# Expert slots taken in pairs of a big and a small one, phase by phase, with fewer rows in all, and one test ahead of the overflow loop

## What is computed

```python
def swiglu(h, w_gate, w_up, w_down):
    return (jax.nn.silu(h @ w_gate) * (h @ w_up)) @ w_down

def moe_swiglu(h, router_w, w_gate, w_up, w_down):      # h: 256 tokens x 1024
    logits = xt @ router_w                               # 8 experts
    top_val, top_idx = lax.top_k(logits, 2)
    top_w = softmax(top_val)
    # each token goes through its two experts: 1024 -> 3584 (gate, up), silu(gate) * up, 3584 -> 1024
    # out[token] = sum over its two experts of top_w * swiglu(token)
    ...
x = x + g_f * moe_swiglu(...)
return rms_norm(x, final_g)
```

## Time and profile before

| | us |
|---|---|
| median of three runs | 1509.3 (1508.0 to 1511.3) |
| the profiled execution | 1512.6 |
| its span, first to last instruction | 1510.8 |
| TensorE busy | 1430.1 |
| VectorE / ScalarE busy | 405.9 / 304.2 |

### The profile page before, as it was taken

The page is one execution under the profiler, slowest core; times in us unless marked ns, Lnnn a source line. Parts: engine busy times, 40 slices in busy tenths (PEclk is TensorE's granted clock), DMA queues, the critical chain, the costliest instruction groups (busy, mean ns, idle before and its releaser), DMA issues.

```text
span 1510.8 us, 26562 instructions
## 1 busy us (share of the span) xinstructions
PE 1430.1 (95%) x11666; PEld 724.1 (48%) x11667; DVE 405.9 (27%) x759; ACT 304.2 (20%) x556; POOL 36.6 (2%) x86
## 2 busy tenths in 40 slices
PE   6999999999999989999977899999999999999795
PEld 5757888887685772343322333334333343333231
DVE  4867655554496651100000000000100000000003
ACT  2356444433235420010100100001010010001001
POOL 1011000000000200000000000000000000000010
PEclk9999999999999989999999999999999999999999
DMA  9988574555757978999999999766999999995796
GB/s 350 312 346 293 181 230 172 208 205 216 267 212 309 326 310 298 383 371 403 403 409 409 402 408 409 295 236 225 407 402 409 409 402 409 408 362 209 294 404 250
DMA packets 149166, 489.31 MB, mean 324 GB/s; under 512 B 9562, under 2 KB 12066, under 8 KB 143938
## 3 DMA queue, kind: packets, MB, share of 16 engines
q1 hardware_dynamic: 141922, 475.06, 81.7%
q10 hardware_dynamic: 5328, 8.05, 1.9%
q0 software_dynamic: 1808, 4.60, 1.0%
HBM read 479.42 MB, written 6.16 MB: 321 GB/s over the span
## 4 chain that ended last, share of the span: by engine, by line
PE 77%; SPq 10%; DMA 6%; DVE 4%; ACT 2%; issue 2%; POOL 0%; DVEq 0%; POOLq 0%; ACTq 0%
PE ps L2322 31%; PE ps L2362 14%; PE ps L2041 7%; PE ps L2043 7%; PE ps L2042 7%; SPq L704 6%; SPq L710 3%; DMA raw<-in_moe_w_down_dram 2%; DMA weights<-in_ada_w_dram 2%; PE ps L2294 1%; PE ps L1967 1%; DMA raw<-in_moe_w_up_dram 1%; DVE weights_lo L1200 1%; PE ps L2339 1%; PE ps L2122 1%
## 5 line engine op out<-in xcount | busy, mean ns | idle before, releaser
L2322 PE MATMUL ps<-raw,hX 128*32 128x512 f32 (+1 forms) x5248 | 570.9, 592 | 27.2 <-DMA raw<-in_moe_w_up_dram 17.3
L2322 PEld LDWEIGHTS ps<-raw,hX 128*32 128x32 f32 x5248 | 168.4, 111 | 403.3 <-issue 370.7
L2362 PE MATMUL ps<-raw,m_actT 128*32 128x512 f32 x2240 | 248.8, 592 | 12.8 <-DMA raw<-in_moe_w_down_dram 12.0
L2041 PE MATMUL ps<-weights_hi,hT_hi 128*128 128x512 f32 (+1 forms) x416 | 162.1, 390 | 2.6 <-DVE hT_lo L1303 1.4
L2043 PE MATMUL ps<-weights_hi,hT_lo 128*128 128x512 f32 (+1 forms) x416 | 159.0, 382 | 0.0
L2042 PE MATMUL ps<-weights_lo,hT_hi 128*128 128x512 f32 (+1 forms) x416 | 158.7, 381 | 0.0
L2362 PEld LDWEIGHTS ps<-raw,m_actT 128*32 128x32 f32 x2240 | 72.8, 110 | 175.9 <-issue 163.3
L1596 DVE TENSOR_TENSOR m_act<-m_sg,ps 128x512 f32<-128x512 f32 (+2 forms) x32 | 23.5, 735 | 465.5 <-ACT m_sg L1034 465.5
L1200 DVE TENSOR_TENSOR weights_lo<-weights,weights_hi 128x2048 fp32r<-128x2048 f32 (+1 forms) x52 | 113.1, 2202 | 2.3 <-ACT weights_hi L873 1.1
L1594 DVE TENSOR_TENSOR m_actX<-m_sgX,ps 128x256 f32<-128x256 f32 (+1 forms) x12 | 4.7, 388 | 368.4 <-ACT m_sg L1034 368.4
L873 ACT ACTIVATE weights_hi<-weights 128x2048 fp32r<-128x2048 f32 (+1 forms) x48 | 87.2, 1839 | 55.6 <-PE ps L2043 51.3
(11 more groups left out here) (246 smaller groups left out, 1017.1 us busy)
## 6 DMA issues: line engine op xcount, KB each, us to landing
raw<-in_moe_w_gate_dram SPq DMA_DIRECT2D x112, 1024.0 KB, 15.4
raw<-in_moe_w_up_dram SPq DMA_DIRECT2D x112, 1024.0 KB, 17.9
raw<-in_moe_w_down_dram SPq DMA_DIRECT2D x112, 1024.0 KB, 16.1
weights<-in_ada_w_dram SPq DMA_DIRECT2D x20, 2048.0 KB, 9.8
weights<-in_ffn_w_gate_dram SPq DMA_DIRECT2D x14, 1024.0 KB, 6.3
weights<-in_ffn_w_up_dram SPq DMA_DIRECT2D x14, 1024.0 KB, 8.9
weights<-in_ffn_w_down_dram SPq DMA_DIRECT2D x7, 2048.0 KB, 10.4
weights<-in_w_in_dram SPq DMA_DIRECT2D x6, 2048.0 KB, 12.6
```

Of the source, the lines that this page charges most:

```text
L2041: pe.matmul(dst, stat_hi, hi, start=start, stop=False, skip_group_check=True)
L2322: mm = pe.matmul(ps[32 * q:32 * q + 32, bank, 0:2 * w].rearrange("p (g n) -> p g n", g=2), hX[:, z.rows_at, k, at32:at32 + 32], weights[:, ...
L2362: mm = pe.matmul(ps[32 * quarter:32 * quarter + 32, DOWN_BANK[c], 0:w], stationary[:, 32 * half:32 * half + 32], raw[buffer][:, D * j + w ...
```

## The change

The slots become "A", "ABX", "X", "AX", "X", "AB", "A", "A": eight wide passes and four X passes, 640 rows. Rank 1 (the largest expert) sits in slot 1 (160 rows), ranks 6 and 7 in the X slots 2 and 4 (32 rows), rank 3 in slot 3 (96), rank 2 in slot 5 (128), ranks 4 and 5 in slots 6 and 7 (64), rank 0 in slot 0 (64).

The slots are put in groups, (0), (1, 2), (3, 4), (5, 6), (7). Within a group the two slots are taken phase by phase in turn; `STEPS` lists the 32 steps, and the down sums of a step come behind the unit sums of the next step, which now belongs to the other slot. `chunk_order` follows, with the same 168 chunks and the same nine buffers. A group's rows are gathered and modulated together (up to 192 rows), so there are five gathers for eight before. PSUM banks of the down sums are given out by `DOWN_AT`; an X slot shares bank 7 with its partner, in the other half. Waits on semaphores count steps in place of slots and phases.

`MAX_OVER` is 5. Ahead of the overflow loop every engine loads one flag and skips the whole loop where it is 0.

```diff
-MAX_OVER = 4
+MAX_OVER = 5
-SLOT_RANK = (0, 4, 5, 1, 6, 3, 2, 7)
-SLOT_PASSES = ("AX", "A", "A", "ABX", "A", "AX", "AB", "A")
+SLOT_RANK = (0, 1, 6, 3, 7, 2, 4, 5)
+SLOT_PASSES = ("A", "ABX", "X", "AX", "X", "AB", "A", "A")
+GROUPS = ((0,), (1, 2), (3, 4), (5, 6), (7,))
-DOWN_BANK = {"A": 5, "B": 6, "X": 7}
+DOWN_AT = ({"A": (5, 0)}, {"A": (5, 0), "B": (6, 0), "X": (7, 0)}, {"X": (7, HU)}, {"A": (5, 0), "X": (7, 0)},
+           {"X": (7, HU)}, {"A": (5, 0), "B": (6, 0)}, {"A": (7, 0)}, {"A": (5, 0)})
+DOWN_FREE = (0, 1, 0, 3, 0, 4, 5, 6)
+GATHER_BANKS = ((2, 3, 6, 7), (0, 1, 2, 3), (0, 1, 2, 3), (4,))
+STEPS = [(s, n) for group in GROUPS for n in range(NPH) for s in group]
+def step_before(s, n):
+    p = STEPS.index((s, n))
+    return [STEPS[p - 1]] if p and (s, n) != (LAST, 0) else []
+def ended_by(s, n):
+    return step_before(s, n) + ([(s, n)] if n == NPH - 1 and s >= LAST - 1 else [])
 def chunk_order():
     order = []
-    for s in range(N_EXP):
-        for n in range(NPH):
-            order += [("gu", s, n, i) for i in range(GU_CHUNKS[n])]
...
+    for s, n in STEPS:
+        order += [("gu", s, n, i) for i in range(GU_CHUNKS[n])]
+        for t, m in ended_by(s, n):
+            order += [("down", t, m, i) for i in range(DOWN_CHUNKS[m])]
     return order
...
             def down_sums(sig, z, n):
-                pe.wait_ge(sig.copied, z.s * NPH + (n + 1))
-                if n == 0 and sig is main and z.s:
-                    pe.wait_ge(sig.y, z.s)
+                pe.wait_ge(sig.copied, z.at(n))
+                if n == 0 and z.down_free:
+                    pe.wait_ge(main.y, z.down_free)
+                if n == NPH - 1 and not z.starts:
+                    pe.wait_ge(main.y, z.s)
...
-            def slot(s):
-                z = MainSlot(s)
+            def step(s, n):
+                z, j = MainSlot(s), GROUP_OF[s]
...
-                pe.wait_ge(main.rows, s + 1)
-                unit_sums(main, z, 0)
-                if s not in (0, LAST):
-                    down_sums(main, MainSlot(s - 1), NPH - 1)
-                turn_units(main, z, 0)
-                for n in range(1, NPH):
-                    unit_sums(main, z, n, (next_rows if s < LAST else last_picks) if n == NPH - 1 else None)
-                    down_sums(main, z, n - 1)
-                    turn_units(main, z, n)
-                if s >= LAST - 1:
-                    down_sums(main, z, NPH - 1)
+                if (s, n) == (GROUPS[j][0], 0):
+                    pe.wait_ge(main.rows, j + 1)
+                ends = n == NPH - 1 and s == GROUPS[j][-1]
+                unit_sums(main, z, n, (next_rows if s < LAST else last_picks) if ends else None)
+                for t, m in step_before(s, n):
+                    down_sums(main, MainSlot(t), m)
+                turn_units(main, z, n)
+                if n == NPH - 1 and s >= LAST - 1:
+                    down_sums(main, z, n)
             def overflow():
-                with pe.Fori(0, MAX_OVER) as o:
-                    used = pe.value_load(table[0:1, 1, bass.ds(o, 1)], min_val=0, max_val=1)
-                    with pe.If(used > 0):
+                any_over = pe.value_load(table[0:1, 1, 0:1], min_val=0, max_val=1)
+                with pe.If(any_over > 0):
+                    with pe.Fori(0, MAX_OVER) as o:
+                        used = pe.value_load(table[0:1, 1, bass.ds(o, 1)], min_val=0, max_val=1)
+                        with pe.If(used > 0):
...
```

More of the change, by code:

```diff
@@ L542, in wide_passes, with gathered_at @@
             return sum(c != "X" for c in passes)
[L544 to L549, removed]
+        def gathered_at(n, banks, k):
             per = 512 // n
@@ L1091, in overflow @@
[L1091 to L1101 removed]
+                if n == NPH - 1 and s == GROUPS[GROUP_OF[s]][-1]:
+                    if s < LAST:
+                        modulated_group(GROUP_OF[s] + 1, GATHER_BANKS[GROUP_OF[s]])
+                    else:
+                        act.wait_ge(turned_pick, 1)
+                        act.activation(pickT[:], ps[:, 2, 0:NT * P].rearrange("p (t n) -> p t n", t=NT),
+                                       ACT.Copy).then_inc(pick_copied, 1)
@@ new lines, in step @@
+                silu(main, z, n)
+                turned_units(main, z, n)
+                for t, m in ended_by(s, n):
+                    if m == NPH - 1 and t < LAST:
+                        store_main(t)
+            def overflow():
+                any_over = act.value_load(table[0:1, 1, 0:1], min_val=0, max_val=1)
+                with act.If(any_over > 0):
+                    with act.Fori(0, MAX_OVER) as o:
+                        used = act.value_load(table[0:1, 1, bass.ds(o, 1)], min_val=0, max_val=1)
+                        with act.If(used > 0):
+                            z = OverSlot(o)
+                            modulated_rows(over, o + 1, z.rows_at, OVER_CAP, OVER_GATHER)
+                            for n in range(NPH):
+                                silu(over, z, n)
+                                turned_units(over, z, n)
+                            store_rows(over, z, lambda r, n, cols: y_over[bass.ds(o, 1), r:r + n, cols].rearrange(
+                                "a p n -> p (a n)"))
@@ L1103, in experts @@
             def experts():
                 act.wait_ge(gate_ff, 8 * 16 * DEPTH)
-                modulated_rows(main, MainSlot(0), (2, 3))
-                for s in range(LAST):
-                    slot(s)
-                act.wait_ge(table_ready, 1)
-                overflow()
-                slot(LAST)
+                modulated_group(0, FIRST_GATHER)
+                for s, n in STEPS:
+                    if (s, n) == (LAST, 0):
+                        act.wait_ge(table_ready, 1)
+                        overflow()
+                    step(s, n)
@@ L2414, in experts @@
-            def experts():
-                gather(main, MainSlot(0), (2, 3))
-                for s in range(LAST):
-                    slot(s)
-                pe.wait_ge(table_ready, 1)
-                overflow()
-                slot(LAST)
+                if (s, n) == (GROUPS[j][0], 0):
+                    pe.wait_ge(main.rows, j + 1)
+                ends = n == NPH - 1 and s == GROUPS[j][-1]
+                unit_sums(main, z, n, (next_rows if s < LAST else last_picks) if ends else None)
@@ L2421, in experts @@
+            def experts():
+                gather(main, 1, GROUP_CAP[0], FIRST_GATHER)
+                for s, n in STEPS:
+                    if (s, n) == (LAST, 0):
+                        pe.wait_ge(table_ready, 1)
+                        overflow()
+                    step(s, n)
                 pe.wait_ge(pick_copied, 1)
```

291 lines of the change are left out of this document (136 added, 155 removed).

## The result

The changed kernel takes 1426.5 us in the median (1426.1 to 1427.4, four runs) beside 1509.5 us for the kernel before on the same chip. The ratio is 0.945, with a 95% interval of 0.943 to 0.947: 83 us are gone. The forecast was 1423.5 us, the range 1408 to 1450.

A forecast was written before the change was run, and what follows sets the result against it. TensorE and DMA transfers bound in turns, transfers next: start 569.5, plus 832 of transfer, 7 of stall, 1.5 landing, about 1410; tail 14.9 gives span 1425, corrected by 1.8 and 3.3 to 1423.5 us; range 1408 to 1450.

The forecast's parts named there:

- The bound: In the expert stage TensorE and the DMA engines take turns; with TensorE at 770 us, under 836, transfers bound next.
- The removed work: In the expert stage 112 us of products and some 11 us of gathers go; TensorE's 893.5 us become about 770.
- The stream: Weight transfers start at 569.5 us, take 832 us and stand about 7 us; the last chunk has landed at 1410.
- The groups: TensorE against 216 us of transfers: (ABX, X) 243, (AX, X) 163 with some 12 us of waits, (AB, A) 235.
- The tail: From the last chunk's start to the end of the span: 14.9 us, unchanged.
- The test: Flag check ahead of the last slot: some 2 us left of 7.02 us idle; the saving counts nothing in the sum.
- Start at half clock: TensorE's first piece of the stage: about 5.9 us at 1.2 GHz, the first chunk ending near 568.3 us.
- edges dearer than thought: Rival: each of eight step edges in group (ABX, X) exposes 5 us instead of 2; 1447 us, chance 0.12.
- rival 2: TensorE idles between X chunks in group (AX, X), which runs wholly at 1.2 GHz: 1480 us, chance 0.03.
- Slower transfers: Rival: over the stage the mean rate is no better than 363 GB/s; kernel ends at 1518 us, chance 0.03.
- The rooms: Rival: an expert has more rows than its slot's room, so an overflow slot AB runs: 1597 us, chance 0.01.
- the pairs level nothing: Rival: order in the groups fails, slots alternate as before, only some 50 us fall: 1460 us, chance 0.03.

## Why the prediction was right

*The bound.* That the two resources took turns, and that the transfers would be next, held: fewer products changed nothing, fewer bytes 61 us. *The removed work.* 112 us of products and 11 of gathers were forecast to go, 123 in all; TensorE's busy time fell by 111, and in the stage it was 783 us for 770. That 111 stands so near the 112 is chance. The gathers gave back 9 us (27.4 to 18.6), and about 15 us of the changed kernel's busy time is half clock, as the kernel with fewer bytes showed, which I had priced mostly as a rival. It had no effect on the end, since TensorE's work was no longer the bound. *The stream.* Start at 569.5, 832 us of transfer, a stall of 7, landing near 1410: TensorE's wait for the last chunk ended at 1410.7. Inside that sum two terms were off, one each way, and that they cancelled is luck. The stall was about 3 us (one slice of 35.6 us at 376 GB/s beside 409), since the group (ABX, X) took 234.9 us for the 243 forecast: of its eight edges only the four into a small step exposed a wait, 1.0 to 1.5 us each (row 1 below), 5.6 us in all for the 16 forecast. The transfers took that much longer: 339.0 MB in some 841 us, 403 GB/s, or some 405 without the stall, for the 407.5 forecast.

```profile
683.30 7.07 PE L2353 MATMUL ps<-raw,hX 128*32 128x512 f32 x64 [1.54 <-ACT m_actT L1080]
...
954.37 1.92 PE L2353 MATMUL ps<-raw,hX 128*32 128x512 f32 x16 [3.17 <-DMA raw<-in_moe_w_up_dram]
959.48 3.55 PE L2353 MATMUL ps<-raw,hX 128*32 128x512 f32 x16 [3.19 <-DMA raw<-in_moe_w_up_dram]
```

*The groups.* TensorE's waits in (AX, X) were forecast as 12 us and came to 29. The sum by whole groups overlooks that the lead swings inside a group: an X step eats it, the next big step builds it up again. I let TensorE enter the group with a full lead of 41 us. But the lead was full when the stream stopped, near 808 us, and the quick X chunks behind that ate part of it: from 877.4 us to its first wait for a chunk, ended at 949.3, TensorE read 18 chunks while some 14 landed at 5.15 us each, so it entered with about five chunks, 26 us, an estimate from these rows. That the lead would be gone at the end of the group held: the next group's first wait for a chunk came after nine more chunks and ended at 1121.9, 46.7 us in. The waits cost nothing, since the stream didn't stop. *The tail.* 15.0 us for 14.9. *The test.* Its gap was 4.5 us for the 2 forecast, and the size was wrong; that it wouldn't count was right. *Start at half clock.* The first piece took 16.8 us for 13.9, as reckoned, and the two kernels with an earlier start show that this is on the path.

Of the rivals: edges dearer than thought, no, they were cheaper. The clock: it did fall, as rival 2 feared, in single chunks (row 3 above: 3.55 us for the 1.92 of the row ahead of it); the slack covered it. The Trainium skill, TensorE: Matmul & The Clock Gate, section HAM oscillation, names this pattern, and the trace agrees in kind, though not each starved chunk ran at half clock (row 2 above, 1.92 us behind a wait of 3.17); it moved the end by nothing here. Slower transfers: the mean was 403 GB/s over 841 us. The Trainium skill, DMA: Bandwidth & Descriptors, section Where 436 GB/s comes from, has about 358 GB/s as the limit; the measurement differs, and that figure doesn't bind this core running alone. The rooms held. That the pairs level nothing was refuted by the kernel without pairs; that kernel took 1483.9 us, so the 1460 which I gave for this rival was 24 us too low.

## What to carry to other kernels

Where two engines each look nearly full over a stage, make the table by stretch: if they take turns at being full, the buffer between them is too small for the unevenness, and ordering big and small work in finer turns can give more than taking work away (55 against 28 us here). Once a stream of transfers sets the end, only what starts it sooner, stops it less or makes it smaller counts; 3 to 5 us at its first chunk are worth more than 72 us of products. Price an edit by the stage it sits in: the same test was worth 5.8 us in one kernel and nothing in the other.

## What the runs showed of the hardware

Chunks whose products take 1.9 us, each met by a wait of 3.2 us, ran partly at 1.2 GHz: 3.55 and 3.6 us beside others at 1.92, in the changed kernel; in the kernel without pairs the granted clock over the stretch of its first X slot was 0.90, with 407 GB/s moved.

One turn of a loop that loads a flag and skips its body costs TensorE about 1.6 us, by the differences above. Behind the 7.0 us gap of four such turns the next piece started at half clock, 15.82 us for 13.94; behind 4.5 us it took 15.28, behind 10.8 us 16.45, and behind a gap of 2.2 us 13.94.
